# Opening by tiles of the model's width inside the first projection; query norms applied as scales of the exponential

## The chip, the cores and the metric

One core of a Trainium2 chip runs the whole program. The metric is the device time in microseconds, the median of several executions. TensorE (PE) multiplies into PSUM, VectorE (DVE), ScalarE (ACT) and GpSimd (POOL) do elementwise work, and SyncE (SP) and ScalarE issue DMAs. Each engine runs its own instructions in order; they wait for each other by semaphores.

## The reference

Two layers over 1024 latent tokens and 256 context tokens of width 1024. Each layer modulates its input by shifts and scales made from two conditions (one for latents, one for context), projects it, mixes by windowed attention (group A), global attention (group B) and a state-space scan, projects out, and ends with a gated feed-forward part. What matters here:

```python
mod = jax.nn.silu(c) @ w_ada[l] + b_ada[l]          # latents
mod_c = jax.nn.silu(c_ctx) @ w_ada[l] + b_ada[l]    # context
sh1, sc1, g1, sh2, sc2, g2 = jnp.split(mod[:, None, :], 6, axis=-1)
y, yc = hybrid_mixer(x * (1 + sc1) + sh1, ctx * (1 + csc1) + csh1, ...)

# group B: queries and keys are divided by their root mean square over a head
out_b = global_block_attention(
    apply_axial_rope(rms_norm(to_heads(bq), q_gain), cos, sin),
    apply_axial_rope(rms_norm(to_heads(bk), k_gain), cos, sin), to_heads(bv), cbk, cbv)
# s = (q * 64 ** -0.5) @ k_all ; p = softmax(s) ; out = p @ v_all
```

The last layer returns latents only, so its context stream needs neither the attention's output nor gates or feed-forward.

## The kernel before

Activations lie feature-major: eight tiles of 128 features by 1280 tokens, the tokens in chunks of 512, 512 and 256 columns. Matmuls are done in three passes, with each operand split into a rounded high part and a low part. A stage is one block of engine programs; `end_stage` closes it with a barrier. The stages around the change are these.

`load_inputs` (L315) is the first stage. SyncE loads the 16 tiles of modulation weights for shift and scale, the input `x` and the constants. VectorE does two products with a sum per tile (L284), one for each condition, then adds the bias (L297) and one to the scales (L300).

`project_attention` (L472) follows, with `modulate_inputs` (L348) ahead of it in the first layer. That lead modulates each tile of `x` on VectorE (L366), rounds it on ScalarE (L378), forms the low part on VectorE or GpSimd in turn (L357, L387), scales `x` (L370) and spills it to memory from ScalarE's queue. TensorE waits for all eight tiles. Then come eight blocks of 128 output columns: two of queries, keys and values, for group A and then for group B. Each block walks the chunks in the order 2, 0, 1, and inside a chunk all eight tiles. A `Ring` holds two blocks of weights. The first two are rounded on ScalarE (L417) with the low parts on VectorE (L424); the others are split by GpSimd in two passes (L432, L434) when the block two before is done. ScalarE evicts each chunk (L556). The value blocks are transposed (L466) and copied out by VectorE (L577), or rounded by ScalarE (L562) with a remainder on VectorE (L582). In VectorE's program half of the 64 other modulation products of the layer stand before the copies of the first value block, and half behind them; TensorE may start its next block's transposed banks and go on only behind these copies.

`norm_and_rotate` (L589) loads the rotary table, then normalises three tiles (two of queries, one of keys, group B) chunk by chunk: square on ScalarE (L647), sum on TensorE (L688), root on ScalarE (L663), reciprocal (L715) and multiplication (L718) on VectorE. Twelve half-tiles are turned: TensorE rotates (L680), the products with cosine (L703) are GpSimd's, the products with sine (L627) and the addition (L631) are GpSimd's for group A and VectorE's for group B.

`attend` (L728) goes over units of one head and one tile of 128 queries, group A and then group B. VectorE takes the maximum of the scores (L1000) and its negative times the scale (L1004 for A, L1007 for B), ScalarE the exponential (L1081), TensorE transposes it (L942) and multiplies by values. There are 64 units of group B over 1280 keys in the two layers.

Of the kernel before, what the change touches and what calls it, by code (L numbers as in the profile page):

```python
# [113 lines left out]
class Plan:  # L114


    def __init__(self, nc, ctx, arrays):
# [8 lines left out]
        self.dtr = at("dtr", [P, TT, 2 * CH], F32, low=12544)  # L126
        self.small = at("small", [P, 32], F32, low=13312)
# [8 lines left out]
        self.x = at("x_res", [P, KT, TOK], F32, kb=80)  # L136
        self.qk = at("qk", [P, 6, TOK], F32, kb=80)
# [38 lines left out]
class Lead:  # L176
# [5 lines left out]
    def __init__(self, ready, tensor, scalar, vector, gpsimd=None, sync=None, prm_free=None):  # L182
        self.ready, self.prm_free = ready, prm_free
        self.tensor, self.scalar, self.vector = tensor, scalar, vector
        self.gpsimd = gpsimd or (lambda pool: None)
        self.sync = sync or (lambda sp: None)
# [49 lines left out]
class Modulation:  # L236
# [6 lines left out]
    def __init__(self, pl, l, first, end, scale_tiles):  # L243
# [31 lines left out]
    def sums(self, dve, r):  # L275

        n = self.SLOTS
        for s in range(n):
# [4 lines left out]
            for c, done in ((0, self.first_done), (1, self.tile_done)):  # L283
# [3 lines left out]
                if c == 0:  # L287
                    dve.wait_ge(done, r * n + (s + 1))

    def finish(self, dve):  # L290

        pl, count = self.pl, self.end - self.first
        dve.wait_ge(self.bias_in, 16)
        dve.wait_ge(self.tile_done, count + self.SLOTS)
        part = pl.mod[:, self.first:self.end, :]
        bias = pl.bada[:, self.first:self.end].unsqueeze(2).broadcast_to([P, count, 2])
# [11 lines left out]
def other_modulation(pl, l):  # L308

    return Modulation(pl, l, G1, 6 * KT, SC2)  # L310
# [4 lines left out]
def load_inputs(pl):  # L315
    nc, a = pl.nc, pl.a
    loaded = pl.sem("start_loaded")
    ada = first_modulation(pl, 0)
    with nc.Block() as block:
        @block.sync  # L320
        def _(sp):
            ada.start(sp)

            with sp.Fori(0, G1 // ada.SLOTS) as r:
                ada.load(sp, r)
                for j in range(2):
                    sp.dma_start(pl.x[:, r * 2 + j, :], a["xT"][:, r * 2 + j, :]).then_inc(loaded, 16)
            sp.dma_start(pl.const[:, :], a["consts"]).then_inc(loaded, 16)
            sp.wait_ge(loaded, 16 * (KT + 1))

        @block.scalar
        def _(act):
            ada.silu(act)

        @block.vector
        def _(dve):
            dve.memset(pl.small[:, 0:1], RMS_EPS)
            dve.memset(pl.small[:, 1:2], LN_EPS)
            dve.memset(pl.small[:, 2:3], 1.0)
            dve.wait_ge(ada.cond_ready, 1)  # L340
            with dve.Fori(0, G1 // ada.SLOTS) as r:
                ada.sums(dve, r)
            ada.finish(dve)

def modulate_inputs(pl):  # L348

    tmp = [pl.at(f"modt{s}", [P, TOK], F32, kb=148 + 5 * s) for s in range(3)]  # L350
    scaled, rounded, kept, spilled = (pl.sem(f"mod_{x}") for x in ("scaled", "rounded", "kept", "spilled"))
    rest = [pl.sem(f"mod_rest{s}") for s in range(2)]

    def vector(dve, between):
        def rest_of(k):
            dve.wait_ge(rounded, k + 1)
            dve.tensor_tensor(pl.lo[:, k, :], tmp[k % 3][:, :], raw(pl.hi[:, k, :]), ALU.subtract) \  # L357
                .then_inc(rest[1], 1)
        for k in range(KT):
            if k == 2:  # L360
                between()
            if k >= 3:

                dve.wait_ge(rest[(k - 3) % 2], (k - 3) // 2 + 1)
            for (t0, t1), who in (((0, SEQ), 0), ((SEQ, TOK), 1)):
                dve.tensor_scalar(tmp[k % 3][:, t0:t1], pl.x[:, k, t0:t1],  # L366
# [4 lines left out]
            if k >= 2 and k % 2 == 0:  # L371
                rest_of(k - 1)
# [99 lines left out]
def project_attention(pl, l, last, lead):  # L472
# [22 lines left out]
    with nc.Block() as block:  # L495
        @block.sync
        def _(sp):
# [11 lines left out]
            for r in (6, 7):  # L509
                ada.load(sp, r)  # L510
# [2240 lines left out]
```

## Time and profile before

| | us |
|---|---|
| median of three executions (3722.94 to 3726.32) | 3723.15 |
| profiled execution | 3726.16 |
| its span | 3724.4 |
| TensorE, VectorE, GpSimd, ScalarE busy | 3313.6, 1985.8, 1449.6, 885.8 |

The profile is of one execution. Busy time is given by engine; a window line gives it for a stretch of the span; a timeline line gives start, duration, engine, line of the kernel, tiles out<-in and, in brackets, the idle time before it and what ended it. The granted clock is 1.00 where TensorE has 2.4 GHz throughout. TensorE is busy in nine tenths or more of most slices of the span, but not in the first slice, and less in the slices of the rotate stages, of the start of the second layer and of the scans.

### The profile page before, as it was taken

The page shows a single profiled execution, that of the slowest core. Times are in us where ns is not written, and L with a number is a line of the kernel's source. Part 1 is how long each engine was busy: PE and PEld are TensorE (multiplying, and loading weights), DVE is VectorE, ACT ScalarE, POOL GpSimd, SP SyncE. Part 2 cuts the span into 40 slices and gives each one's busy share as a digit, 9 for nine tenths or more (in the row PEclk, how much of TensorE's full clock was granted, in tenths as well). Part 3 has the DMA queues.
Part 4 walks back from the last instruction along what each step waited for, and adds up shares of the span by engine and source line. Part 5 has one row for each costly group of instructions (what it writes and reads, how often), then busy time and mean ns, then how long its engine had stood idle before and what let it go on. Part 6 is the DMA issues. An engine that isn't in the chain of part 4 may idle for free. (4 is left out here: it accounts for less than half of the span.)

```text
span 3724.4 us, 47054 instructions
## 1 busy us (share of the span) xinstructions
PE 3313.6 (89%) x16840; PEld 2754.3 (74%) x16840; DVE 1985.8 (53%) x2984; ACT 885.8 (24%) x1715; POOL 1449.6 (39%) x1052
## 2 busy tenths in 40 slices
PE   0969989887999999999997678989788899999997
PEld 0849878655878888888885558978666688888884
DVE  7986844678474233332227886845686732121225
ACT  1136742212131000000003226742211310000002
POOL 1344222253444343344332244222244554445443
PEclk9979999978999999999998788999889999999998
DMA  7400011002112121122111420011003111111111
GB/s 284 164 29 1 1 43 54 6 20 76 63 40 74 62 67 62 56 68 73 39 34 57 169 79 1 1 45 53 6 14 105 56 51 45 51 45 51 51 46 50
DMA packets 70621, 213.63 MB, mean 57 GB/s; under 512 B 6768, under 2 KB 17776, under 8 KB 69488
## 3 DMA queue, kind: packets, MB, share of 16 engines
q1 hardware_dynamic: 59040, 179.67, 14.4%
q10 hardware_dynamic: 11472, 32.53, 2.5%
q8 instruction: 66, 1.08, 0.1%
q14 instruction: 43, 0.35, 0.0%
HBM read 192.78 MB, written 19.40 MB: 57 GB/s over the span
## 5 line engine op out<-in xcount | busy, mean ns | idle before, releaser
L196 PE MATMUL ps<-h_hi,f_whi 128*128 128x512 f32 (+1 forms) x1760 | 650.9, 370 | 3.5 <-DVE f_gated L2597 3.5
L197 PE MATMUL ps<-h_lo,f_whi 128*128 128x512 f32 (+1 forms) x1760 | 649.1, 369 | 0.0
L198 PE MATMUL ps<-h_hi,f_wlo 128*128 128x512 f32 (+1 forms) x1760 | 648.4, 368 | 0.0
L2597 DVE TENSOR_TENSOR f_gated<-f_gated,ps 128x512 f32<-128x512 f32 (+1 forms) x110 | 69.6, 634 | 821.5 <-PE ps L198 820.2
L2423 POOL TENSOR_TENSOR f_whi<-f_wraw,small 128x1024 fp32r<-128x1024 f32 x130 | 247.6, 1905 | 558.9 <-PE ps L198 529.5
L2606 DVE SCALAR_TENSOR_TENSOR x_res<-ps,mod,x_res 128x512 f32<-128x512 f32 (+1 forms) x440 | 306.7, 697 | 242.4 <-PE ps L198 241.8
L196 PEld LDWEIGHTS ps<-h_hi,f_whi 128*128 128x128 f32 x1760 | 332.6, 189 | 61.3 <-DVE f_gated L2597 3.9
L197 PEld LDWEIGHTS ps<-h_lo,f_whi 128*128 128x128 f32 x1760 | 332.6, 189 | 55.9 <-issue 1.0
L198 PEld LDWEIGHTS ps<-h_hi,f_wlo 128*128 128x128 f32 x1760 | 332.4, 189 | 55.6
L2425 POOL TENSOR_TENSOR f_wlo<-f_wraw,f_whi 128x1024 fp32r<-128x1024 f32 x130 | 327.0, 2515 | 10.2
L196 PE MATMUL ps<-f_ahi,f_whi 128*128 128x512 f32 (+1 forms) x880 | 328.2, 373 | 0.0
L197 PE MATMUL ps<-f_alo,f_whi 128*128 128x512 f32 (+1 forms) x880 | 323.5, 368 | 0.0
L198 PE MATMUL ps<-f_ahi,f_wlo 128*128 128x512 f32 (+1 forms) x880 | 323.4, 367 | 0.0
L2537 ACT ACTIVATE f_gated<-ps 128x512 f32<-128x512 f32 (+1 forms) x110 | 61.0, 556 | 904.7 <-PE ps L198 671.3
L2448 POOL TENSOR_TENSOR f_alo<-f_gated,f_ahi 128x512 fp32r<-128x512 f32 (+1 forms) x110 | 134.2, 1221 | 352.1 <-ACT f_ahi L2544 352.1
L284 DVE SCALAR_TENSOR_TENSOR ada_product<-ada_w,ada_cond 128x1024 f32<-128x1024 f32 x160 | 231.1, 1444 | 42.9 <-ACT ada_cond L273 12.1
L196 PE MATMUL ps<-h_hi,whic 128*128 128x512 f32 (+1 forms) x592 | 215.4, 364 | 14.8 <-DVE wloc L424 14.8
L196 PE MATMUL ps<-h_hi,whiab 128*128 128x512 f32 (+1 forms) x352 | 130.4, 371 | 109.0 <-DVE h_lo L357 89.7
L197 PE MATMUL ps<-h_lo,whic 128*128 128x512 f32 (+1 forms) x592 | 213.4, 360 | 0.0
L198 PE MATMUL ps<-h_hi,wloc 128*128 128x512 f32 (+1 forms) x592 | 213.2, 360 | 0.0
L196 PEld LDWEIGHTS ps<-f_ahi,f_whi 128*128 128x128 f32 x880 | 165.3, 188 | 30.8 <-DVE x_res L2606 0.2
L197 PEld LDWEIGHTS ps<-f_alo,f_whi 128*128 128x128 f32 x880 | 165.6, 188 | 27.6
(257 smaller groups left out, 6525.7 us busy)
## 6 DMA issues: line engine op xcount, KB each, us to landing
f_wraw<-in_w_ffn SPq DMA_DIRECT2D x130, 512.0 KB, 3.5
ada_w<-in_w_ada SPq DMA_DIRECT2D x80, 512.0 KB, 3.6
later_w<-in_w_ada ACTq DMA_DIRECT2D x32, 512.0 KB, 3.5
o_wraw<-in_w_out SPq DMA_DIRECT2D x28, 512.0 KB, 3.5
wrawc<-in_w_in SPq DMA_DIRECT2D x26, 512.0 KB, 3.8
wrawab<-in_w_in SPq DMA_DIRECT2D x16, 512.0 KB, 4.1
x_res<-x_spill SPq DMA_DIRECT2D x6, 1024.0 KB, 8.0
x_res<-in_xT SPq DMA_DIRECT2D x8, 640.0 KB, 7.3
```

The lines of the kernel that those rows point to most:

```text
L196: pe.matmul(out, w_hi, h_hi, start=first, stop=False)
L197: pe.matmul(out, w_hi, h_lo, start=False, stop=False)
L198: return pe.matmul(out, w_lo, h_hi, start=False, stop=last)
L284: dve.scalar_tensor_tensor(out=self.product[:, :], in0=self.w[s][:, :], scalar=1.0, in1=self.cond[:, c, :], op0=ALU.mult, op1=ALU.mult, ac ...
L2423: pool.tensor_tensor(hi, w.raw[par][:, :], one, ALU.mult).then_inc(rounded, 1)
L2425: pool.tensor_tensor(lo, w.raw[par][:, :], raw(hi), ALU.subtract).then_inc(ready, 1)
L2448: pool.tensor_tensor(act_lo[:, f, t0:t0 + tn], gated[f][:, t0:t0 + tn], raw(act_hi[:, f, t0:t0 + tn]), ALU.subtract).then_inc(act_in[c], 1)
L2537: act.activation(gated[f][:, t0:t0 + tn], pl.bank(c, tn), ACT.Silu) \
L2597: dve.tensor_tensor(g, g, pl.bank(3 + c, tn), ALU.mult).then_inc(u_taken[c], 1)
L2606: dve.scalar_tensor_tensor(out=x, in0=pl.bank(6 + d % 2, tn), scalar=pl.mod[:, G2 + n, who:who + 1], in1=x, op0=ALU.mult, op1=ALU.add).the ...
```

## The change

1. The first stage only sets three columns of constants, on GpSimd. `first_inputs` becomes the lead of the first projection: VectorE makes the shift and the scale of one tile of the width, ScalarE modulates, rounds, scales and spills that tile, VectorE forms its low part, and TensorE does blocks 0 and 1 together, tile after tile (`multiply_along`). The other modulation products of the layer follow, two rounds of four tiles before the copies of the first value block and six behind them.
2. From block 2 on ScalarE rounds the weights after its evictions, and GpSimd forms the low part only. This holds for both layers.
3. In the last layer the later modulation products are made for one condition only.
4. The rotary table is loaded by SyncE at the end of the projection, to a place of its own.
5. Group B's queries are turned without being normalised, with the gain in the product with cosine and in a rotation matrix of its own. Their sums of squares go, two columns a tile, to one PSUM bank; their inverse roots become `q_scale`, which the attention uses for the maximum and as the exponential's scale. GpSimd turns group A wholly and VectorE group B wholly.

```diff
+def first_inputs(pl):
+    ada = Modulation(pl, 0, SH1, 6 * KT, SC2)
+    order = [tile for k in range(KT) for tile in (SH1 + k, SC1 + k)]
...
+    def sync(sp, ring_loads):
+        ada.start(sp)
+        for n, tile in enumerate(order):
+            s = n % ada.SLOTS
+            sp.wait_ge(ada.tile_done, n + 1)
+            sp.dma_start(ada.w[s][:, :], a["w_ada"][0, tile]).then_inc(ada.w_in[s], 16)
+            if n % 2 == 1:
+                k = n // 2
+                sp.dma_start(pl.x[:, k, :], a["xT"][:, k, :]).then_inc(x_in[k], 16)
+                if k < 2:
+                    ring_loads[k]()
+        sp.dma_start(pl.const[:, :], a["consts"]).then_inc(consts_in, 16)
...
         for k in range(KT):
+            product(2 * k)
+            product(2 * k + 1)
+            dve.wait_ge(ada.tile_done, 2 * k + 2 + ada.SLOTS)
...
+            dve.tensor_tensor(part, part, bias, ALU.add).then_inc(biased, 1)
+            if k >= 1:
+                rest_of(k - 1)
             if k == 2:
                 between()
+        rest_of(KT - 1)
+        dve.wait_ge(consts_in, 16)
+
+    def scalar(act, between):
+        ada.silu(act)
+        for k in range(KT):
+            act.wait_ge(biased, k + 1)
+            act.wait_ge(x_in[k], 16)
             if k >= 3:
+                act.wait_ge(rest, k - 2)
             for (t0, t1), who in (((0, SEQ), 0), ((SEQ, TOK), 1)):
+                act.activation(tmp[k % 3][:, t0:t1], pl.x[:, k, t0:t1], ACT.Identity,
+                               bias=pl.mod[:, SH1 + k, who:who + 1],
+                               scale=pl.mod[:, SC1 + k, who:who + 1]).then_inc(scaled, 1)
             act.wait_ge(scaled, 2 * k + 2)
             act.activation(pl.hi[:, k, :], tmp[k % 3][:, :], ACT.Copy).then_inc(rounded, 1)
+            act.activation(pl.x[:, k, :], pl.x[:, k, :], ACT.Copy, scale=ALPHA).then_inc(kept, 1)
             act.wait_ge(kept, k + 1)
             act.dma_start(pl.x_dram[:, k, :], pl.x[:, k, :]).then_inc(spilled, 16)
+            if k == 0:
+                between()
         act.wait_ge(spilled, KT * 16)
...
+def multiply_along(pl, pe, ring, chunks, full, taken, tiles_in):
+    for c in ORDER:
+        pe.wait_ge(taken[c], 2)
+    pe.wait_ge(ring.ready, 4)
+    for k in range(KT):
+        pe.wait_ge(tiles_in, k + 1)
+        for n in range(2):
+            for c in ORDER:
+                if c in chunks[n]:
+                    t0, tn = CHUNKS[c]
+                    mm = three_pass(pe, pl.bank(3 * n + c, tn), ring.hi[n][:, k, :], ring.lo[n][:, k, :],
+                                    pl.hi[:, k, t0:t0 + tn], pl.lo[:, k, t0:t0 + tn], k == 0, k == KT - 1)
+                    if k == KT - 1:
+                        mm.then_inc(full[c], 1)
...
-    return Modulation(pl, l, G1, 6 * KT, SC2)
+    return Modulation(pl, l, G1, 6 * KT, SC2, conditions=1 if l == DEPTH - 1 else 2)
...
             def body(at):
+                evict(at)
+                if at.n < 6:
+                    act.wait_ge(full[1], at.n + 3)
+                    ring.round_block(act, at.n + 2)
...
-            over(pool, [(3, ["w", "w"])], lambda kind: (), lambda at: ring.split(pool, at, full[1]), start=2)
+            over(pool, [(3, ["w", "w"])], lambda kind: (), lambda at: ring.rest(pool, at), start=2)
...
+            sp.wait_ge(full[1], 6)
+            sp.wait_ge(stored, 4)
+            sp.dma_start(pl.rope[:, :, :], a["rope"]).then_inc(table_in, 16)
+            sp.wait_ge(table_in, 16)
...
+            for i, (r0, r1) in enumerate(((0, first_rounds), (first_rounds, 8))):
+                with dve.Fori(r0, r1) as j:
+                    ada.sums(dve, j + begun)
...
+            key_norm(0)
+            key_norm(1)
+            turn(0)
+            key_norm(2)
+            for m in range(1, 4):
+                turn(m)
+            if not last:
+                for t in (3, 4):
+                    dve.wait_ge(squared, squares.index((t, 2)) + 1)
+                    x = pl.qk[:, qk_slot(t), SEQ:TOK]
+                    dve.tensor_scalar(x, x, gain_q, None, ALU.mult)
+            for m in range(4, 6):
+                turn(m)
+            dve.wait_ge(q_rooted, 1)
+            n = q_tiles * HEADS
+            dve.reciprocal(inv_q[:, 0:n], root_q[:, 0:n]).then_inc(q_inverted, 1)
...
             def maximum(w):
+                if w.group == 1:
+                    dve.tensor_copy(q_scale[w.h], pl.q_scale[:, 0, w.i, w.h:w.h + 1])
...
-                    dve.tensor_scalar(nm[w.h], mx[w.h], -SCALE, None, ALU.mult).then_inc(nm_done, 1)
+                    at_tile = pl.q_scale[:, :, w.i, w.h]
+                    dve.tensor_tensor(nm[w.h], mx[w.h], at_tile[:, 1:2], ALU.mult).then_inc(nm_done, 1)
...
                 act.activation(prob[w.par][:, 0:n_keys[w.kind] * P], w.scores(), ACT.Exp, bias=nm[w.h],
-                               scale=SCALE, accum_out=den[w.h]).then_inc(p_done, 1)
+                               scale=SCALE if w.group == 0 else q_scale[w.h],
+                               accum_out=den[w.h]).then_inc(p_done, 1)
```

The norm-and-rotate stage's other new functions, in short: TensorE sums each key chunk as before (`key_sum`), and each query chunk by one matmul per 128 tokens with two columns of output (`query_sums`, 20 in the first layer, 16 in the second). Its program sets them in one order with the rotations `rotate_a` (group A) and `rotate_b` (group B). In `turn` VectorE multiplies with cosine, multiplies the rotated half out of PSUM with sine, and adds; the addition waits until ScalarE has squared the chunk.

## Rows read from the trace of the kernel before

**Rows 1.** Windows: length, busy us by engine (instructions), granted clock, DMA share, GB/s.
```profile
0.00:53.80 53.80, 0.00 (x0) 0.00 (x0) 39.94 (x69) 3.19 (x2) 0.20 (x4) 1.00 0.81 295
...
89.70:209.20 119.50, 114.74 (x596) 98.84 (x596) 101.22 (x136) 15.94 (x28) 33.01 (x12) 1.00 0.41 142
209.20:257.30 48.10, 26.20 (x42) 10.31 (x42) 43.75 (x30) 14.07 (x25) 31.97 (x25) 0.75 0.06 23
...
366.00:492.00 126.00, 124.32 (x917) 112.21 (x916) 111.42 (x218) 93.81 (x185) 36.93 (x64) 1.00 0.00 1
...
2195.20:2238.20 43.00, 22.81 (x38) 7.96 (x38) 38.16 (x26) 12.72 (x21) 32.21 (x25) 0.78 0.07 24
```

**Rows 2.** Timeline, VectorE, opening: start us, us, engine, line, out<-in, [idle <-releaser].
```profile
8.36 1.23 DVE L284 SCALAR_TENSOR_TENSOR ada_product<-ada_w,ada_cond 128x1024 f32<-128x1024 f32 x1 [7.42 <-DMA ada_w<-in_w_ada]
...
52.36 0.19 DVE L297 TENSOR_TENSOR mod<-mod,b_ada 128x32 f32<-128x32 f32 x1
...
54.00 1.14 DVE L366 TENSOR_SCALAR modt<-x_res,mod 128x1024 f32<-128x1024 f32 x2 [1.24 <-PEq L159]
...
87.90 1.49 DVE L357 TENSOR_TENSOR h_lo<-modt,h_hi 128x1280 fp32r<-128x1280 f32 x1 [0.47 <-ACT h_hi L378]
```

**Rows 3.** Timeline, TensorE's first matmul, and ScalarE after its last spill.
```profile
89.69 0.55 PE L196 MATMUL ps<-h_hi,whiab 128*128 128x256 f32 x1 [89.69 <-DVE h_lo L357]
...
90.41 1.91 ACT L273 ACTIVATE ada_cond<-ada_cond 128x2048 f32<-128x2048 f32 x1 [2.54 <-DMA x_spill<-x_res]
```

**Rows 4.** Timeline, first projection: GpSimd's second pass, a product beside it, ScalarE's evictions.
```profile
121.40 3.25 POOL L434 TENSOR_TENSOR wloab<-wrawab,whiab 128x1024 fp32r<-128x1024 f32 x1
...
122.57 3.17 DVE L284 SCALAR_TENSOR_TENSOR ada_product<-ada_w,ada_cond 128x1024 f32<-128x1024 f32 x1 [0.16 <-DVE ada_product L284]
...
122.09 0.38 ACT L556 ACTIVATE qk<-ps 128x256 f32<-128x256 f32 x1 [2.27 <-PE ps L198]
...
135.88 0.39 ACT L556 ACTIVATE ab_vst<-ps 128x256 f32<-128x256 f32 x1 [2.27 <-PE ps L198]
...
151.60 0.39 ACT L556 ACTIVATE qk<-ps 128x256 f32<-128x256 f32 x1 [4.22 <-PE ps L198]
...
204.35 0.38 ACT L562 ACTIVATE v_b<-ps 128x256 fp32r<-128x256 f32 x1
...
209.25 0.94 ACT L647 ACTIVATE nr_sq<-qk 128x256 f32<-128x256 f32 x2 [2.18 <-PEq L159]
```

**Rows 5.** Timeline, second layer's first projection: ScalarE's evictions, VectorE's copy.
```profile
2084.27 0.38 ACT L556 ACTIVATE qk<-ps 128x256 f32<-128x256 f32 x1 [0.28 <-PE ps L198]
...
2145.53 0.60 ACT L556 ACTIVATE qk<-ps 128x512 f32<-128x512 f32 x1 [35.96 <-PE ps L198]
...
2136.00 0.42 DVE L577 COPY v_a<-ps 128x256 f32<-128x256 f32 x1
```

**Rows 6.** Timeline, VectorE in the first norm-and-rotate stage.
```profile
212.01 1.75 DVE L715 RECIPROCAL nr_ri<-nr_rt 128x256 f32<-128x256 f32 x1 [3.76 <-ACT nr_rt L663]
...
217.91 1.85 DVE L718 SCALAR_TENSOR_TENSOR qk<-qk,prm,nr_ri 128x512 f32<-128x512 f32 x1
219.69 3.34 DVE L715 RECIPROCAL nr_ri<-nr_rt 128x512 f32<-128x512 f32 x1
...
249.95 1.33 DVE L631 TENSOR_TENSOR qk<-nr_xc,nr_xs 128x512 f32<-128x512 f32 x1
...
255.83 0.69 DVE L631 TENSOR_TENSOR qk<-nr_xc,nr_xs 128x512 f32<-128x512 f32 x1
```

**Rows 7.** Timeline, VectorE, one unit of the global attention.
```profile
424.48 1.49 DVE L1000 TENSOR_REDUCE at_st<-ps 128x1 f32<-128x1280 f32 x1
426.01 0.15 DVE L1007 TENSOR_SCALAR at_st<-at_st 128x1 f32<-128x1 f32 x1
...
428.53 1.49 DVE L1000 TENSOR_REDUCE at_st<-ps 128x1 f32<-128x1280 f32 x1
```

**Rows 8.** Groups of instructions by line and shape: count, busy us, mean ns of one.
```profile
L718 DVE SCALAR_TENSOR_TENSOR qk<-qk,prm,nr_ri 128x512 f32<-128x512 f32 x12 | 11.5, 961 | 0.4
```

More of the change, by code:

```diff
@@ L308, in other_modulation @@
 def other_modulation(pl, l):
-    return Modulation(pl, l, G1, 6 * KT, SC2)
[L315 to L343, printed above, removed]
@@ L348, in modulate_inputs, with set_small, _ @@
-def modulate_inputs(pl):
-    tmp = [pl.at(f"modt{s}", [P, TOK], F32, kb=148 + 5 * s) for s in range(3)]
-    scaled, rounded, kept, spilled = (pl.sem(f"mod_{x}") for x in ("scaled", "rounded", "kept", "spilled"))
-    rest = [pl.sem(f"mod_rest{s}") for s in range(2)]
-    def vector(dve, between):
+    return Modulation(pl, l, G1, 6 * KT, SC2, conditions=1 if l == DEPTH - 1 else 2)
+def set_small(pl):
+    with pl.nc.Block() as block:
+        @block.gpsimd
+        def _(pool):
+            pool.memset(pl.small[:, 0:1], RMS_EPS)
+            pool.memset(pl.small[:, 1:2], LN_EPS)
+            pool.memset(pl.small[:, 2:3], 1.0)
@@ L498, in _ @@
             load = lambda at: ring.load(sp, at, a["w_in"][l, at.n])
-            over(sp, [(1, ["w", "w"])], lambda kind: (), load)
-            ada.start(sp)
+            first = [lambda n=n: load(At(n, n, "w", 0, n, 0, 0)) for n in range(2)]
+            if lead.ada:
+                lead.sync(sp, first)
+            else:
+                first[0]()
+                first[1]()
+                ada.start(sp)
             if lead.prm_free is not None:
@@ L592, in norm_and_rotate @@
     tag = f"nr{l}"
-    norms = [(t, c) for t in (3, 4, 5) for c in ORDER if not (last and t < 5 and c == 2)]
-    turns = [(t, c) for t in range(6) for c in (0, 1)]
-    rope = pl.at(f"{tag}_rope", [P, 2, SEQ], F32, kb=161)
+    K = 5
+    q_parts = [(t, c) for t in (3, 4) for c in ORDER if not (last and c == 2)]
+    squares = [(K, c) for c in ORDER] + q_parts
+    q_tiles = LT if last else TT
+    turns_a = [(t, c) for t in range(3) for c in (0, 1)]
+    turns_b = [(t, c) for t in range(3, 6) for c in (0, 1)]
+    N, NK = len(squares), len(ORDER)
+    rope = pl.rope
     sq = [pl.at(f"{tag}_sq{s}", [P, 512], F32, kb=169 + 2 * s) for s in range(2)]
@@ L689, in _, with query_sums @@
                           stop=True).then_inc(summed, 1)
-                if n < 6:
-                    rotate(n)
-            for n in range(6, len(turns)):
-                rotate(n)
+            def query_sums(n):
+                t, c = squares[n]
+                t0, tn = CHUNKS[c]
+                pe.wait_ge(squared, n + 1)
+                halves = pl.c(BLOCK64).rearrange("p (h d) -> p h d", h=2)[:, :, 0]
+                for j in range(tn // P):
+                    first = (t0 // P + j) * HEADS
+                    out = pl.bank(6)[:, first:first + HEADS].rearrange("p (h k) -> p h k", k=2)[:, :, t - 3]
+                    mm = pe.matmul(out, sq[n % 2][:, j * P:(j + 1) * P], halves, start=True, stop=True)
+                mm.then_inc(summed, 1)
@@ L695, in _ @@
+            b = 0
+            for n in range(N):
+                if n < NK:
+                    key_sum(n)
+                else:
+                    query_sums(n)
+                if n < len(turns_a):
+                    rotate_a(n)
+                if n >= 1 and b < 4:
+                    rotate_b(b)
+                    b += 1
+            for m in range(N, len(turns_a)):
+                rotate_a(m)
+            for m in range(b, len(turns_b)):
+                rotate_b(m)
         @block.gpsimd
```

279 lines of the change are left out of this document (167 added, 112 removed).

## The prediction

> **What bounds the kernel now.** I first read busy time by stretches [rows 1]. In the first layer's projection TensorE is busy 114.74 of 119.5 us; the norm-and-rotate stages, 48.1 and 43.0 us, are VectorE's, with 43.75 and 38.16; in the global attention TensorE is busy 124.32 of 126.0 and VectorE 111.42. Most of the span is untouched, and a barrier ends each stage, so each changed stage is summed by itself and the savings add. The timelines name the waits. VectorE's 32 modulation products run from 8.36 to the bias add at 52.36, 1.372 us each by starts [rows 2]; some 36 us of modulating follow, and TensorE's first matmul comes at 89.69 behind VectorE's last low part [rows 3]. In the second layer the next block's first eviction after the v block comes at 2145.53 after 35.96 us of idle: TensorE waits for VectorE's copies out of PSUM, which stand behind 32 products and come at 2136.00 [rows 5].
>
> **The opening and the first projection.** The old first stage shrinks to three memsets and a barrier of 1.3 us (1.24 before 54.00, [rows 2]), so the first product goes from 8.36 to 9.7. Then VectorE does, per tile of the width, four products, one bias add (0.2, with its wait 0.3) and the low part of the tile before (1.49, by starts 1.45). To the last bias add: 9.7 + 43.9 + 8 x 0.3 + 6 x 1.45 + 2.5 for two weight remainders of about 1.2 each, as a product = 67.2. ScalarE's two modulations and the rounding, 1.1 + 0.4 + 1.4 (its 1.91 for 2048 columns [rows 3] gives 1.0 for 1024, more with operands), reach 70.1, the last low part 71.6. ScalarE's other work per tile (some 4.5 us in all) fits VectorE's 7.2. The DMAs of these 57 us are some 20 MB, 350 GB/s; the first stretch shows 295 at a busy share of 0.81, so 364 if full [rows 1]. I take them as hidden, with a rival below.
>
> A block takes 13.79 us by starts of evictions, 122.09 to 135.88, and 15.72 with the v transposes [rows 4]. TensorE has meanwhile done seven tiles of two blocks; the eighth is 2 x 13.79 / 8 = 3.4, or 6.9 at 1.2 GHz. Neither decides, for now **block 2's weights are late**. ScalarE rounds them in program order behind its wait for the spill (2.54 at the end of the old one, [rows 3]: to about 75) and behind block 0's evictions (1.6): 76.7; rounding 1.1, GpSimd's remainder 3.25 [rows 4]: 81.1. Before, GpSimd did both passes under block 1. Two blocks from 81.1, plus 1.4 for a start at 1.2 GHz (the granted clock falls to 0.75 of 2.4 GHz in the rotate stage, where TensorE has holes, [rows 1]), end at 110.1. VectorE has finished its first 16 products by 98 and waits; transposes and copies end at 112.9. Then 48 products of 1.385 = 66.5. A product beside GpSimd's second pass took 3.17, not 1.23 [rows 4]; that pass stays, the first goes to ScalarE; three blocks fall in this stretch, 2.0 each: 185.4. TensorE's four blocks are done by 168, so VectorE ends the stage now. The tail from the first v_b to the next stage was 204.35 to 209.25 [rows 4]: **190.3 against 209.25, minus 18.9**. Bounds 12 and 24, from the contention (0 to 3.4 a block) and from TensorE's third block (77 to 86). The rope table's load is issued some 11 us before the last product, which hides it; without that cover its 1 MB costs 4 us at the 295 GB/s of rows 1.
>
> **Second layer's projection.** The last layer needs one condition, so 32 products go. Sixteen, of 1.4 to 1.8 us with their loads (four slots of 512 KB), end by 2112. Block 2's rounding moves behind ScalarE here too. Its first eviction stood at 2084.27, so it began near 2081.5. Now: ScalarE comes from its silu at 2082.0, two evictions 1.1, rounding 1.1, remainder 3.25: 2087.5. **6 us are lost**, and the v block, whose last eviction began at 2108.9, ends at 2114.9. The copies follow at once; the next eviction comes 1.9 + 5.4 later and 0.7 for a slow clock, at 2122.9 instead of 2145.53, and from there nothing changes: 22.6, and with 0.5 by which the last product held the first v_b, **minus 23.1**. Bounds 17 (rounding 5 later) and 28 (hidden).
>
> **Norm and rotate.** Removed: six (layer two: four) of nine (seven) reciprocals and their multiplications; moved: the table's load, and six turns go wholly to VectorE. VectorE in layer one: start 2.8 (212.01 less 209.25); three reciprocals 1.75 + 2 x 3.34 = 8.4; their multiplications 2.5; six turns of a multiplication 0.94, one out of PSUM 0.7 and an addition 1.25 = 17.4, less 1 once GpSimd is done; rotation matrix, context scalings and last factors 1.9 [rows 6, 8]. Sum 32. For waits on TensorE, whose rotations stand in one queue with twenty new query sums, 1.5; for whole GpSimd operations waited out, as the 1.85 at 217.91, 1; boundary 0.8: 35.3. GpSimd's six turns of about 4.2 (before, three operations of some 1.3) end by 30. **48.1 to 35.3: minus 12.8; layer two, without context scalings, 43.0 to 34.4: minus 8.6.** Bounds 31 and 42 for each. No row shows the query sums: between the 0.14 of a TensorE instruction in the attention and the 0.62 of one in this stage (busy over count, rows 1) each, 3 to 12 us beside VectorE's 32; I take the low end, as they write two columns.
>
> The turns' two-input operations now run beside GpSimd's: an addition there took 1.33, alone 0.69 [rows 6]. The Trainium skill, "SBUF — State Buffer", section "Who interferes with whom", says that a VectorE instruction with two SBUF inputs and a GpSimd one that reads SBUF exclude each other for a whole instruction. The trace agrees as far as 1.33 against 0.69 goes; by that rule the turns could wait longer, which is the second rival.
>
> **Attention.** Per unit of the global group VectorE gets a copy of one column, and a two-input operation for a one-input one (0.15, [rows 7]). ScalarE's exponential takes a column as scale, which I cost at nothing: ScalarE is busy 93.81 of 126.0. VectorE's units are 4.05 apart [rows 7]; busy it is 3.58 a unit, with some 0.27 of waits on its own results. The copy, which no row shows, costs between 0.07 (issue alone) and 0.3; I take 0.15, the row nearest to it, and 0.06 for the second input: 4.06, at the edge. With address arithmetic 0.05 x 64 units: **plus 3**; bounds 0 and 0.27 x 64 = 17.
>
> **Sum.** 18.9 + 23.1 + 12.8 + 8.6 - 3 = 60.4. The profiled execution took 3726.16 us (span 3724.4), which gives 3665.8; it lies 3.0 above the median of 3723.15, which gives **3662.8**.
>
> **The rivals.**
> Feed: DMAs bound the opening, each tile of the width 9 us and not 7.2: 14 later, 3677. Against it: the loads run two tiles ahead.
> Port: eight more whole GpSimd operations (1.26) waited out per rotate stage, 20 us: 3683. For it: the 1.85 row; against: reciprocals and PSUM reads leave room.
> Attention on VectorE, 0.27 a unit: 14 more, 3677.
> Layer two not freed: if one condition's products wait for their loads (2.8 us a tile, as two products take now), the copies stay near 2136 and 23 us are missing: 3686. The part would then not do what it says.
> Slower than before: VectorE's column copy, with an address out of a register, stalls its queue in each of 64 units. It decides from 60.4 / 64 = 0.94 us a unit more than I gave; at 1.1 the time is 3733. Nothing in the rows is near: the unit's other small operation takes 0.15.
>
> **How the numbers follow.** Forecast 0.64, feed 0.09, port 0.10, attention 0.09, layer two 0.07, slower 0.01. The low end takes 4 off the opening, 4 off each rotate stage, 3 off attention and 3 of the late rounding: 3645. The high end takes in feed, port and attention: 3684. A measurement of this kernel tells about 0.2% (7 us) from no change. Faster 0.98, same 0.01, slower 0.01.
>
> **What would show it.** First matmul near 35, first eviction near 75, a TensorE hole until 81, and the stage's end on VectorE near 190; in layer two no 36 us eviction gap, but a hole of 6 after the second block; rotate stages of 35 and 34 us with four long reciprocals in place of twelve; global units 4.05 to 4.1 apart. It is wrong if TensorE starts the third block after 86, or if the units go over 4.2.

## The result and the profile after

The changed kernel takes 3665.59 us (median of four executions, 3664.91 to 3668.51), the kernel before 3724.02 in four executions beside it (3722.94 to 3726.32): ratio 0.984, 95% interval 0.983 to 0.986. The profiled execution has a span of 3666.7 us against 3724.4. Predicted were 3662.8, in a range of 3645 to 3684.

I split both spans at the first instruction of each stage; the lengths in us, worked out so from the timelines:

| stage | before | after | moved | predicted |
|---|---|---|---|---|
| opening and first projection | 209.3 | 185.0 | -24.3 | -18.9 |
| norm and rotate, layer one | 48.0 | 36.3 | -11.7 | -12.8 |
| attention, layer one | 256.1 | 260.7 | +4.6 | attention together +3 |
| output projection, layer one | 156.7 | 149.1 | -7.6 | 0 |
| first projection, layer two | 113.3 | 91.8 | -21.5 | -23.1 |
| norm and rotate, layer two | 42.9 | 34.6 | -8.3 | -8.6 |
| attention, layer two | 227.9 | 236.4 | +8.5 | |
| the state-space projections and scans, four stages | 753.5 | 757.0 | +3.5 | 0 |

The rest differs by less than 1 us. The +3.5 of the last line is no more than the scatter of that code: it is the same in every kernel of this text, and the four stages took 752.9 to 757.0 us in their fourteen profiles. Busy time by stretches of the changed kernel (columns as in [rows 1]): opening up to the last low part, first projection, rotate stage, a stretch of attention, rotate stage of layer two.

```profile
0.00:65.50 65.50, 27.87 (x119) 22.40 (x120) 53.84 (x84) 38.42 (x36) 0.37 (x7) 0.96 0.95 367
70.60:184.90 114.30, 88.93 (x455) 76.25 (x453) 86.96 (x130) 19.30 (x33) 17.32 (x6) 0.89 0.46 154
185.00:221.30 36.30, 26.05 (x70) 14.80 (x70) 31.70 (x31) 11.37 (x21) 26.34 (x19) 0.69 0.00 1
...
335.00:461.00 126.00, 124.26 (x884) 108.72 (x883) 112.02 (x238) 93.26 (x179) 34.62 (x60) 1.00 0.00 0
...
2135.20:2169.80 34.60, 24.99 (x62) 13.01 (x62) 30.98 (x28) 10.64 (x18) 26.65 (x18) 0.70 0.00 1
```

The rotate stages are still VectorE's, 31.70 of 36.3. In the attention, 31 us earlier than the stretch of before, TensorE is busy 124.26 of 126.0 us as in [rows 1], but with 884 matmuls and not 917. So its busy time doesn't show that a unit got slower; the count does (-3.6%, give or take records that a trace can lack).

The timeline of the opening, in the order in which the steps come (VectorE's first product; TensorE's first matmul; the last bias addition and the last low part; block 0's evictions, block 2's rounding and low part, TensorE's third block, its first eviction; VectorE's copies; TensorE's last eviction; the end):

```profile
8.46 1.23 DVE L365 SCALAR_TENSOR_TENSOR ada_product<-ada_w,ada_cond 128x1024 f32<-128x1024 f32 x1 [1.63 <-ACT ada_cond L279]
29.57 0.55 PE L201 MATMUL ps<-h_hi,whiab 128*128 128x256 f32 x1 [29.57 <-DVE wloab L449]
60.79 0.16 DVE L387 TENSOR_TENSOR mod<-mod,b_ada 128x4 f32<-128x4 f32 x1
64.06 1.49 DVE L373 TENSOR_TENSOR h_lo<-modt,h_hi 128x1280 fp32r<-128x1280 f32 x1 [1.70 <-ACT h_hi L407]
70.56 1.36 ACT L638 ACTIVATE qk<-ps 128x256 f32<-128x256 f32 x3 [5.38 <-DMA x_spill<-x_res]
71.79 1.07 ACT L455 ACTIVATE whiab<-wrawab 128x1024 fp32r<-128x1024 f32 x1
72.94 6.16 POOL L461 TENSOR_TENSOR wloab<-wrawab,whiab 128x1024 fp32r<-128x1024 f32 x2 [72.03 <-ACT whiab L455]
75.83 0.58 PE L201 MATMUL ps<-h_hi,whiab 128*128 128x256 f32 x1 [4.64 <-POOL wloab L461]
80.95 0.39 ACT L638 ACTIVATE qk<-ps 128x256 f32<-128x256 f32 x1 [5.89 <-PE ps L203]
105.86 0.42 DVE L659 COPY v_a<-ps 128x256 f32<-128x256 f32 x1 [14.65 <-PE ps L521]
162.65 0.60 ACT L638 ACTIVATE ab_vst<-ps 128x512 f32<-128x512 f32 x1 [4.84 <-PE ps L203]
179.38 0.38 ACT L644 ACTIVATE v_b<-ps 128x256 fp32r<-128x256 f32 x1 [16.14 <-DVE ada_product L291]
184.98 0.94 ACT L718 ACTIVATE nr_sq<-qk 128x256 f32<-128x256 f32 x2 [2.03 <-PEq L161]
```

The path is as forecast: VectorE until 65.5, ScalarE's wait for the spill, the rounding behind it, GpSimd's low part, TensorE's third block (75.83, forecast 81.1). Then VectorE ends the stage: TensorE's last eviction is at 162.65, and the first v_b waits for the last product until 179.38. The second layer's projection, ScalarE and VectorE, which answers to [rows 5]:

```profile
2046.36 1.08 ACT L455 ACTIVATE whiab<-wrawab 128x1024 fp32r<-128x1024 f32 x1
2054.01 0.38 ACT L638 ACTIVATE qk<-ps 128x256 f32<-128x256 f32 x1 [6.57 <-PE ps L203]
2078.69 0.60 ACT L638 ACTIVATE ab_vst<-ps 128x512 f32<-128x512 f32 x1 [4.84 <-PE ps L203]
2078.91 0.42 DVE L659 COPY v_a<-ps 128x256 f32<-128x256 f32 x1 [4.56 <-PE ps L521]
2086.05 0.60 ACT L638 ACTIVATE qk<-ps 128x512 f32<-128x512 f32 x1 [5.82 <-PE ps L203]
```

The idle time of 35.96 us is gone: VectorE waits for the v block now, by 4.56 us. In its place a hole stands before block 2's first eviction: ScalarE is idle for 6.57 us, TensorE for 5.37.

### The profile page after: what moved, and what is told of

It is laid out like the page before. It is cut to its first block and busy times, and to the rows that moved or that the text cites. A ratio compares the mean times of both kernels' runs of the same rounds, so it can differ in the third digit from the quotient of the medians.

```text
span 3666.7 us, 47014 instructions
## 1 busy us (share of the span) xinstructions
PE 3337.3 (91%) x16892; PEld 2773.8 (76%) x16892; DVE 1897.6 (52%) x2978; ACT 920.8 (25%) x1742; POOL 1389.5 (38%) x1027
## 5 line engine op out<-in xcount | busy, mean ns | idle before, releaser
L2590 POOL TENSOR_TENSOR f_wlo<-f_wraw,f_whi 128x1024 fp32r<-128x1024 f32 x130 | 326.9, 2515 | 10.2
L201 PE MATMUL ps<-h_hi,whic 128*128 128x512 f32 (+1 forms) x592 | 216.4, 366 | 14.6 <-DVE wloc L449 14.6
L203 PEld LDWEIGHTS ps<-f_ahi,f_wlo 128*128 128x128 f32 x880 | 165.6, 188 | 27.6
```

What stands on the lines that cost most here:

```text
L201: pe.matmul(out, w_hi, h_hi, start=first, stop=False)
L203: return pe.matmul(out, w_lo, h_hi, start=False, stop=last)
L2590: pool.tensor_tensor(lo, w.raw[par][:, :], raw(hi), ALU.subtract).then_inc(ready, 1)
```

## The experiments

Totals of these kernels can't be compared to better than some 8 us, because one stage of them all, the first output projection, takes either 149.1 or 156.7 us (below). So the verdicts rest on stage lengths, worked out as above from one profiled execution of each kernel. The two medians of a row were taken side by side.

| kernel | median, before beside it | end of first projection | attention, both | output proj. 1 | first proj. 2 |
|---|---|---|---|---|---|
| changed kernel | 3665.6, 3724.0 | 185.0 | 497.1 | 149.1 | 91.8 |
| e1_one_input | 3661.7, 3723.1 | 185.0 | 485.2 | 156.7 | 91.3 |
| e2_constants | 3655.4, 3723.1 | 184.5 | 481.8 | 156.7 | 91.2 |
| e3_copy_kept | 3655.6, 3723.1 | 185.2 | 485.3 | 149.1 | 91.9 |
| e11_two_inputs_fixed_address | 3661.9, 3717.6 | 185.8 | 495.1 | 149.2 | 91.8 |
| e12_one_input_register_address | 3659.0, 3717.6 | 184.9 | 493.5 | 149.1 | 91.8 |
| e4_three_rounds | 3659.2, 3723.1 | 174.8 | 494.7 | 156.7 | 91.2 |
| e5_round_first | 3657.4, 3718.8 | 180.4 | 495.7 | 149.1 | 90.1 |
| e8_gpsimd_both_passes | 3671.1, 3718.8 | 186.7 | 496.2 | 149.1 | 93.1 |
| e7_one_condition_alone | 3699.4, 3718.8 | 208.3 | 484.3 | 149.2 | 93.3 |
| e10_before_split_waits | 3718.1, 3717.6 | 208.8 | 484.1 | 149.1 | 113.8 |
| e9_gpsimd_turns_small | 3661.0, 3718.8 | 184.6 | 495.0 | 149.1 | 91.8 |
| e6_combined | 3636.9, 3717.6 | 171.8 | 483.2 | 149.1 | 90.1 |

**What the attention lost.** It was costed at +3 and lost 13.1. The timeline of two units in the changed kernel, VectorE and GpSimd, and a count of what line L1171 puts on VectorE's sequencer in a longer stretch (least, median and longest duration in ns):

```profile
384.43 0.14 DVE L1161 COPY at_st<-q_scale 128x1 f32 x1
384.64 1.49 DVE L1163 TENSOR_REDUCE at_st<-ps 128x1 f32<-128x1280 f32 x1
386.27 0.16 DVE L1171 TENSOR_TENSOR at_st<-at_st,q_scale 128x1 f32<-128x1 f32 x1
388.84 1.49 DVE L1163 TENSOR_REDUCE at_st<-ps 128x1 f32<-128x1280 f32 x1
390.23 0.74 POOL L1048 TENSOR_TENSOR at_q_two<-at_qst,at_q_two 64x256 fp32r<-64x256 f32 x1
390.47 0.51 DVE L1171 TENSOR_TENSOR at_st<-at_st,q_scale 128x1 f32<-128x1 f32 x1
...
L1171 DVEq FUSED_REGOPS  x19: 57/57/65, 369.0 to 446.1; - x19
```

Units are 4.20 apart here, 4.05 in [rows 7]; on average over both layers 4.21 and 4.01. Three things differ: the copy; the negated maximum starts 1.63 after the maximum, not 1.53 [rows 7], with an instruction on a register of 57 ns ahead of it; and it lasts up to 0.51 where GpSimd stages the next queries. At 390.47 it ends when GpSimd's instruction does, 390.98 and 390.97. Five kernels take these apart.

```diff
# e1_one_input
-                    at_tile = pl.q_scale[:, :, w.i, w.h]
-                    dve.tensor_tensor(nm[w.h], mx[w.h], at_tile[:, 1:2], ALU.mult)
+                    dve.tensor_scalar(nm[w.h], mx[w.h], q_scale[w.h], -1.0, ALU.mult, ALU.mult)
# e2_constants: no copy, scale=SCALE in the exponential, and the line of before:
+                    dve.tensor_scalar(nm[w.h], mx[w.h], -SCALE, None, ALU.mult)
# e3_copy_kept: as e2, with the copy
# e11_two_inputs_fixed_address
+                    dve.scalar_tensor_tensor(out=nm[w.h], in0=mx[w.h], scalar=-1.0, in1=q_scale[w.h], ...)
# e12_one_input_register_address
+                    dve.tensor_scalar(nm[w.h], at_tile[:, 1:2], mx[w.h], None, ALU.mult)
```

> The changed kernel, with the attention's negated maximum made of the copied column and the constant -1, so by an instruction with one streamed input instead of two. The two attention stages took 259.7 and 235.4 us against 255.1 and 226.8 before, 13.2 more together. Theory A, VectorE bounds a unit and each of its three additions counts (copy about 0.2 by starts, second input 0.02 to 0.36, exponential with a column as scale 0.09): the copy stays, so some 3 to 5 us come back, 3661 to 3663. Theory B, the second input is the whole loss, because it waits for GpSimd's staging of the queries: 10 to 13 come back, 3653 to 3656. Theory C, it costs nothing: 3665.

> The changed kernel with the attention stage as it was before: no copy, constant scale in the exponential, negated maximum by a constant. This leaves out the queries' division by their root mean square. If the 13.2 us of the two attention stages are the price of these three edits alone: 3652, and units 4.06 to 4.09 us apart instead of 4.2 to 4.3. If they come from elsewhere (other data placement, the clock), 3665.

> As the one with constants, but VectorE's copy of the column stays in each unit of the global attention, its result unused; the queries' division by their root mean square is left out. If VectorE bounds the unit, the copy costs its 0.2 us by starts in each of some 60 units: 10 to 13 us more than the kernel with constants, some 3663. If it sits in time in which VectorE waits for TensorE's scores anyway, the loss is the second input's and the exponential's: within 3 us of the kernel with constants, 3652 to 3655.

> The changed kernel with the negated maximum as a product of the maximum, -1 and the copied column: two streamed inputs as in the changed kernel, but no address out of a register. If the second input is what costs, the two attention stages take some 497 us together, as there, and the instruction starts 0.14 us after the maximum, up to 0.5 long beside GpSimd's staging: 3665. If the address in a register is what costs: 485, as with one input: 3654.

> The changed kernel with the negated maximum as one streamed column of the table of factors, with its address out of a register, times the maximum's column as the scalar operand. If the second streamed input is what costs: 485 us in the two attention stages, 3654. If the address in a register is what costs: 497, 3665.

Stage lengths are too coarse for these differences. The changed kernel and the four others with its attention code (e4, e5, e8, e9) lie between 494.7 and 497.1, and e2, whose attention code is that of before, is 2.2 us below the 484.0 of before. The 32 global units of a layer, group B's alone, repeat much better. This is the time from the start of the first of their maxima to the start of the last, both layers added (62 intervals), worked out from the timelines:

| negated maximum and copy | kernels | us |
|---|---|---|
| as before, by a constant | before, e7, e10, e2 | 248.7, 248.8, 248.7, 248.4 |
| the same, with the copy | e3 | 249.7 |
| copy, one streamed input, fixed address | e1, e6 (below) | 250.5, 250.6 |
| copy, one streamed input, address in a register | e12 | 257.1 |
| copy, two streamed inputs, fixed address | e11 | 257.4 |
| copy, two streamed inputs, address in a register | changed kernel, e4, e5, e8, e9 | 261.0 to 261.1 |

So 12.4 of the 13.1 us are in these units. The copy costs 1.3. The column as the exponential's scale and the longer form of the negated maximum (0.21 for 0.15) cost 0.8 together. The rest, 10.6, is the instruction of the negated maximum. I had put two theories on record for it, each as the whole cause, and both kernels missed: the second input alone costs 7.0, the register alone 6.7. They add up to 13.6 and cost 10.6 together. The rows of e12 (first two lines) and of e11 (the others):

```profile
383.60 1.49 DVE L1163 TENSOR_REDUCE at_st<-ps 128x1 f32<-128x1280 f32 x1
385.23 0.21 DVE L1171 TENSOR_SCALAR at_st<-q_scale,at_st 128x1 f32 x1
...
382.64 1.49 DVE L1163 TENSOR_REDUCE at_st<-ps 128x1 f32<-128x1280 f32 x1
383.87 0.73 POOL L1048 TENSOR_TENSOR at_q_two<-at_qst,at_q_two 64x256 fp32r<-64x256 f32 x1
384.16 0.46 DVE L1170 SCALAR_TENSOR_TENSOR at_st<-at_st 128x1 f32<-128x1 f32 x1
```

In e12 the start is late (1.63) and the duration short, in e11 the start is on time (1.52) and the instruction lasts until GpSimd's has ended (384.62 and 384.60). That is where the time goes in a unit, and part of the way on can be seen: TensorE's weight loads for the scores waited 8.4 us for VectorE's remainders in the first layer's attention before, and 11.8 us in the changed kernel. Why the two together cost less than their sum wasn't tried.

The Trainium skill, "SBUF — State Buffer", section "Who interferes with whom", says that a VectorE instruction with two SBUF inputs and a GpSimd one that reads SBUF exclude each other for a whole instruction. By that rule even an instruction on one column waits until GpSimd's has ended, and e11's row agrees: it takes 0.46, and 0.16 where nothing holds it.

**The idle 14.65 us.** One number is changed:

```diff
-    first_rounds = 2 if lead.ada else 4
+    first_rounds = 3 if lead.ada else 4
```

> The changed kernel with one number changed: 24 products instead of 16 ahead of VectorE's copies of the first values, in the first layer. VectorE stood idle 14.65 us before these copies, and eight products take 11.1 us. If VectorE sets the stage's end, 11 us go: stage end at 174 instead of 185, 3654.6. If TensorE does, which had its last eviction at 162.7, nothing up to 3 us less would be lost of it: still 3655. If the products are slowed by the weights' remainders on GpSimd, of which more now lie beside them, 8 to 10: 3656 to 3658.

The stage went from 185.0 to 174.8, the total to 3659.2, with the long output projection in its profile. So VectorE's products end the stage, and 10.2 of the 14.65 idle us were for the taking.

**Block 2's late weights.** The first kernel puts block 2's rounding first, the second gives the rounding back to GpSimd. A third, e7, is the kernel before with only the part for one condition:

```diff
# e5_round_first (and the wait for the spill moves behind it)
             def body(at):
+                if at.n == 0:
+                    act.wait_ge(full[1], at.n + 3)
+                    ring.round_block(act, at.n + 2)
+                    if lead.ada:
+                        act.wait_ge(*lead.spilled)
                 evict(at)
# e8_gpsimd_both_passes (and ScalarE's rounding from block 2 on is left out)
-            over(pool, ..., lambda at: ring.rest(pool, at), start=2)
+            over(pool, ..., lambda at: ring.split(pool, at, full[1]), start=2)
```

> The changed kernel with block 2's rounding on ScalarE ahead of the wait for the spill and of block 0's evictions, in both layers. Block 0's last matmul ends near 69.3, so the rounding goes from 71.79 to 69.4, GpSimd's remainder from 72.94 to 70.6, TensorE's third block from 75.83 to 73.7. If the late weights hold the whole chain up to VectorE's copies, which wait for the v block, the stage ends 2.1 earlier, 183; in the second layer the rounding gains the two evictions, 0.9. Together 3 us: 3662.5. If it is something else that ends the wait before block 2: no change, 3665.5.

> The changed kernel with both passes over blocks 2 to 7 back on GpSimd, none on ScalarE. The prediction's theory: in the second layer the hole after the second block (5 to 6 us) goes; in the first layer block 2's weights come 1.5 earlier (rounding from 69.3 on, 3.1 + 3.1, not 76.0), but three more passes lie beside VectorE's 48 products after the copies, up to 1.8 each: stage end 185 - 1.5 + 3 to 5.4 = 187 to 189, in all 3662 to 3664. The other theory, that the first pass costs VectorE nothing and ScalarE's rounding is only late: 3659.

> The kernel before with the last layer's modulation sums over one condition, as in the changed kernel, and nothing else. GpSimd still does both passes over block 2's weights under block 1, so the hole after the second block isn't there. By the prediction's working that part alone gives 23.1 plus the 6 us of the hole, 28 to 29: 3695. If the hole in the changed kernel comes from elsewhere, the stage is 21.6 us shorter, as there: 3702.

e5 gave 4.6 in the first layer where 2.1 was expected. Its rounding, third block and first eviction, its windows 70 to 75 and 75 to 80, and the second window in the changed kernel:

```profile
69.43 1.06 ACT L455 ACTIVATE whiab<-wrawab 128x1024 fp32r<-128x1024 f32 x1 [4.22 <-PE ps L203]
73.11 0.39 PE L201 MATMUL ps<-h_hi,whiab 128*128 128x256 f32 x1 [1.98 <-POOL wloab L461]
76.29 0.38 ACT L643 ACTIVATE qk<-ps 128x256 f32<-128x256 f32 x1 [2.26 <-PE ps L203]
...
70.00:75.00 5.00, 3.02 (x20) 2.46 (x20) 4.71 (x5) 4.03 (x8) 3.38 (x2) 1.00 0.51 179
75.00:80.00 5.00, 5.00 (x29) 4.32 (x28) 4.71 (x5) 0.38 (x1) 1.51 (x1) 1.00 0.24 57
...
75.00:80.00 5.00, 4.17 (x19) 4.17 (x20) 4.86 (x3) 0.05 (x1) 4.10 (x2) 0.50 0.25 94
```

The block starts 2.7 earlier, and it also runs at 2.4 GHz: behind an idle time of 1.98 us the granted clock is 1.00, and the first chunk takes 3.2 us. In the changed kernel TensorE idled 4.64, the clock was 0.50 in 75 to 80 (1.2 GHz), and the chunk took 5.1. So 1.9 of the 4.6 us are the clock's. That the shorter idle time kept the clock up isn't shown: the combined kernel below idles 1.86 us at the same place and doesn't keep it. In the second layer e5 gave 1.7 where 0.9 was expected.

e8 takes 3671.1 us, longer than the changed kernel and above both theories. Without the hole, layer two's stage is 1.3 longer, not 5 shorter. And e7, with GpSimd's two passes too, got 20.0 us off this stage and not 28. The timeline of e8's second layer (last eviction of the v block, the products before the copies, the next eviction):

```profile
2073.62 0.60 ACT L635 ACTIVATE ab_vst<-ps 128x512 f32<-128x512 f32 x1 [4.84 <-PE ps L203]
2074.29 2.40 DVE L291 SCALAR_TENSOR_TENSOR ada_product<-ada_w,ada_cond 128x1024 f32<-128x1024 f32 x1 [0.43 <-DMA ada_w<-in_w_ada]
2076.85 3.12 DVE L291 SCALAR_TENSOR_TENSOR ada_product<-ada_w,ada_cond 128x1024 f32<-128x1024 f32 x1 [0.15 <-DVE ada_product L291]
2079.90 0.41 DVE L656 COPY v_a<-ps 128x256 f32<-128x256 f32 x1
2089.79 0.60 ACT L635 ACTIVATE qk<-ps 128x512 f32<-128x512 f32 x1 [15.57 <-PE ps L203]
```

Counted from the stage's first eviction, TensorE is done with the v block after 27.7 us and not 35.2, but VectorE comes to the copies 6.3 after the last eviction, because its sixteen products now lie beside both passes (six of them took 1.6 to 3.2) and beside their loads. The next block's first eviction is then 43.9 after the first one, in the changed kernel 42.5. e7's stage has the same shape: 27.7 to the end of the v block, 44.0 to the next eviction. The hole and the held products are two prices for the same weights, nearly equal. In the first layer e8 is 1.7 longer: block 2 starts 1.2 earlier (74.62), but five products behind the copies are held instead of three.

**GpSimd beside the turns.** Each operand of GpSimd's turns is cut to one column.

```diff
-                pool.tensor_tensor(xs_a[m % 2][:, :], xs_a[m % 2][:, :], rope[:, 1, t0:t0 + tn], ALU.mult)
+                pool.tensor_tensor(xs_a[m % 2][:, 0:1], xs_a[m % 2][:, 0:1], rope[:, 1, t0:t0 + 1], ALU.mult)
```

> The changed kernel with GpSimd's three operations of each of its six turns on one column in place of 512, so that half of the rotation is left out, and VectorE's turns run alone. If VectorE's two-input operations are held by GpSimd's (1.75 for the multiplications by gain and cosine, 0.94 for the additions, 0.68 for those that are undisturbed), four times 1.07 and six times 0.26 go, some 6 us a stage: 30 and 29, in all 3654. If 1.75 is the operation's own price, under 2 us a stage, 3662.

Measured: 32.7 and 31.7 against 36.3 and 34.6, so 3.6 and 2.9 less, between the two theories. VectorE's groups of instructions in the first rotate stage of the changed kernel (first two lines) and of this one (count, busy us and mean ns, idle time before them):

```profile
L850 DVE SCALAR_TENSOR_TENSOR nr_xcb<-qk,prm,rope 128x512 f32<-128x512 f32 x4 | 7.0, 1750 | 0.0
L861 DVE TENSOR_TENSOR qk<-nr_xcb,nr_xsb 128x512 f32<-128x512 f32 x6 | 5.7, 944 | 1.6 <-ACT nr_sq L718 1.1
...
L851 DVE SCALAR_TENSOR_TENSOR nr_xcb<-qk,prm,rope 128x512 f32<-128x512 f32 x4 | 3.0, 743 | 0.0
L862 DVE TENSOR_TENSOR qk<-nr_xcb,nr_xsb 128x512 f32<-128x512 f32 x6 | 4.2, 692 | 2.9 <-ACT nr_sq L718 2.5
L855 DVE TENSOR_TENSOR nr_xsb<-ps,rope 128x512 f32<-128x512 f32 x6 | 4.1, 684 | 2.7 <-PE ps L767 2.7
```

The mechanism is there: 1750 ns beside GpSimd, 743 alone. VectorE is busy 8 us less (23.49 of 32.7), but less than half of that shortens the stage, since ScalarE's squares and TensorE's rotations are late next.

**The 7.6 us of the output projection, which the change doesn't touch.** VectorE's twelve divisions and GpSimd's first pass over the weights in the first output projection: before (two lines), changed kernel (two), e10 (two).

```profile
911.11 10.83 DVE L2026 TENSOR_SCALAR mix_c<-mix_c,o_rs 128x256 f32<-128x256 f32 x12
912.64 1.89 POOL L1939 TENSOR_TENSOR o_whi<-o_wraw,small 128x1024 fp32r<-128x1024 f32 x1 [27.33 <-DMA o_wraw<-in_w_out]
...
880.80 3.24 DVE L2191 TENSOR_SCALAR mix_c<-mix_c,o_rs 128x256 f32<-128x256 f32 x12
882.84 2.94 POOL L2104 TENSOR_TENSOR o_whi<-o_wraw,small 128x1024 fp32r<-128x1024 f32 x1 [27.83 <-DMA o_wraw<-in_w_out]
...
908.05 3.24 DVE L2028 TENSOR_SCALAR mix_c<-mix_c,o_rs 128x256 f32<-128x256 f32 x12
911.45 1.89 POOL L1941 TENSOR_TENSOR o_whi<-o_wraw,small 128x1024 fp32r<-128x1024 f32 x1 [29.23 <-DVE mix_c L2028]
```

Before, GpSimd starts 1.53 us after the divisions began; it takes 1.89 and they 10.83. In the changed kernel it starts 2.04 after, and it is the one held (2.94). The fourteen profiles fall into two groups: before, e1, e2 and e4 have the first outcome and a stage of 156.7 us, all others a stage of 149.1 or 149.2. The start doesn't decide between them: GpSimd is the one held at 1.64 after (e11) and 1.72 (e8), and VectorE at 1.78 (e1). What decides isn't shown. e10 lets GpSimd wait:

```diff
             def split(p):
                 pool.wait_ge(w_loaded[p % 2], 16 * (p // 2 + 1))
+                if p == 0:
+                    pool.wait_ge(normed[0], len(tiles_of[0]) * GROUPS)
```

> The kernel before with one wait more: in the output projection GpSimd's first split of the weights waits for VectorE's twelve divisions of the mixed values. If the 7.6 us that this stage gave in the changed kernel is a race between these two for the memory port, decided by the weights' landing within some 0.4 us, the divisions take 3.24 us and not 10.83, the stage 149.2 us and not 156.7, and every execution falls by it: 3716. If the stage's length comes from its loads or from TensorE: no gain, or 1 us lost by the later weights, 3724.

The stage is 149.1, as the theory has it, but the median is that of the kernel before, 3718.1 against 3717.6 (ratio 0.9998, interval 0.9989 to 1.0007). The kernel before ran there between 3714.5 and 3724.3, beside e1 to e4, on another chip, nine times between 3722.3 and 3724.8. So the race falls one way or the other in it, and e7, which doesn't touch this stage either, has the 149.2. With the wait none of eleven executions was above 3720.0; without it, on the same chip, 6 of 22 were. So VectorE's and GpSimd's collision is the cause of the 7.6 us, and that it has to do with the change is refuted.

**Together.** e1, e4, e5 and the wait of e10 in one kernel.

> The changed kernel with four edits: the negated maximum by one streamed input (11.7 in the two attention stages), 24 products ahead of the first copies together with block 2's rounding first (the 14.65 us of VectorE's idle time before the copies shrink by 11.1, the v block ends 4.7 earlier, so nearly all of it goes: 14.6), the second layer's rounding first (1.7), and in both output projections GpSimd's first split behind VectorE's twelve divisions (nothing against the profiled execution of the changed kernel, in which the divisions took 3.24 us). 3665.6 - 11.7 - 14.6 - 1.7 = 3637.6. If the products are now bound by their loads or the copies by the products: up to 4 more, 3642.

3636.92 us (3636.21 to 3638.52), ratio 0.978, interval 0.977 to 0.979: 29 us less than the changed kernel, and within 1 of the sum. That it is so close is luck in part: the opening gave 13.1 of its 14.6, and the attention 13.9 where 11.7 was expected. In the opening the clock did not stay up this time:

```profile
73.11 0.39 PE L201 MATMUL ps<-h_hi,whiab 128*128 128x256 f32 x1 [1.86 <-POOL wloab L461]
...
75.00:80.00 5.00, 5.00 (x25) 4.58 (x25) 4.71 (x5) 0.39 (x1) 1.48 (x1) 0.77 0.23 67
```

## Why the prediction was right

The total is 2.8 us off, and all changed stages have the forecast's sign. The mechanism held in the opening, in layer two and in the rotate stages. In the attention it didn't, and one of the prediction's own signs of being wrong came true: the global units are 4.21 apart, where it asked for 4.05 to 4.1 and named 4.2 as too much. That the total is so close is luck: three errors cancel, 5.4 us too little promised for the opening, 10.1 too much for the attention, and 7.6 from a stage that it rightly left at nothing. With the long output projection the changed kernel would have been near 3673, still in the range.

- **Opening**, -18.9 forecast, -24.3 measured. The steps came in the order predicted, each earlier: first matmul 29.57 (35), first eviction 70.56 (75), third block 75.83 (81.1). A tile of the width took 6.6 us and not 7.2: in straight-line code the products are 1.27 to 1.34 apart, not 1.372, and the bias addition is followed after 0.08, not 0.3. The first product came at 8.46, not 9.7, because the condition's silu released it and not the barrier. The last low part ended at 65.5 and not 71.6. Block 2 began at half clock behind the hole, as allowed for. VectorE's 48 last products took 71.0 us, forecast 72.5.
- **Feed rival**: false, but by a narrow margin. The DMAs ran at 367 GB/s and a share of 0.95 until 65.5, and no product waited for them.
- **Layer two**, -23.1 and -21.5; the copies came at once and the next eviction 7.36 after the last of the v block. The step "6 us are lost", the hole, is 7.5 by e8, which is the 1.5 that the forecast was off; e8 and e7 show what the prediction did not see: giving the pass back gains nothing, as VectorE is then held by as much. The rival that the layer isn't freed is false.
- **Norm and rotate**, -12.8 and -8.6, measured -11.7 and -8.3. Inside, a term was mis-sized: a multiplication by gain and cosine was put at 0.94 and took 1.75, four times, held by GpSimd. The additions made up for more than half of it (0.94 where 1.25 was taken, six times), so the stage's close sum is partly luck. The twenty query sums, put at 3 us, kept TensorE busy for 7.4, and VectorE waited for TensorE only 0.3. The port rival has this mechanism; it named 20 us, and e9 gives 6.5 for all of GpSimd's turns in both stages.
- **Attention**, +3 forecast, +13.1 measured, near its bound of 17: the mis-sized term. The copy (0.15) and the second input (0.06) were taken to fit into the unit's waits, and the address arithmetic, 0.05 a unit, made the 3. Measured, the copy costs 1.3 in all, so it mostly fits; the second input and the register together cost 10.6, or 0.17 a unit. So most of the rival "attention on VectorE" (0.27 a unit) came true, which had 0.09. The prediction took these terms as work of an average unit. In the rows they are waits: the second input lasts until GpSimd's instruction has ended, the register moves the start by 0.10. The last rival, slower than before, names the register too, but asks for 0.94 us a unit.
- **Output projection**, 0 forecast, -7.6: not in the change at all. Where the kernel before has the short stage too, the gain is about 50 us and not 58, and the forecast gain of 60.4 is off by 10.
- The +3.5 of state-space projections and scans lies within what the same code scatters by.

## What to carry over

A saving on one engine is worth what the next wait allows, so follow each moved pass to who stands beside it: handing a rounding to ScalarE cost TensorE 7.5 us in the second layer and gave about as much back on VectorE. In a loop whose engine has a quarter of a microsecond of slack, a one-column instruction matters by its form: with one streamed input, a fixed address and the second factor as the scalar operand it cost 10.6 us less here. And before a gain is booked, split the span by stages: a stage that moved without being touched may be a race. Here a wait that orders it cost nothing that could be measured. Where the stages' lengths scatter by more than the effect, count a smaller piece that repeats.

## What the runs showed of the hardware

- Twelve scalings in place of 128x256 took 10.83 us or 3.24, and GpSimd's pass beside them 1.89 or 2.94. In the first case four of them, of 0.35 otherwise, took 1.98 to 2.50, one for each of GpSimd's next four instructions (912.64 to 921.27). In the second, GpSimd's pass let the last four pass first (from 882.90 to 884.04), in e11 the last five. The Trainium skill, "SBUF — State Buffer", section "Who interferes with whom", says of VectorE's modes that use both ports, which such a scaling can enter, that who issues first gets the shared pair for the whole instruction. The four held scalings agree with that; that GpSimd is held over four or five instructions in a row is more than it says. No row shows which mode the scalings were in.
- A short idle time of TensorE left the granted clock up once and not another time: behind 1.98 us it was 1.00 from 75 to 80 (e5), behind 1.86 us at the same place 0.77 (e6). Behind 4.64 us it was 0.50.
- An address out of a register puts 57 ns on the engine's sequencer, and where the instruction also waits for the one ahead of it, its start comes 0.10 us later (1.63 for 1.53).
- Beside GpSimd, a VectorE instruction with two inputs in SBUF took 1750 ns for 743 (gain and cosine, 128x512) and 944 for 692 (addition, 128x512).
